# The head of an 8-core decoder-step kernel: x loads ungated, v's weights in two halves, v's norms in batches

## The reference, cut to what matters

```python
h = rmsnorm(x, g_mix)
proj = h @ w_in
a = proj[..., :o1]                      # pooling branch, 512 columns
z = jax.nn.gelu(proj[..., o1:o2])       # u and v, 512 columns each
u = z[..., :GMLP_WIDTH]
v = rmsnorm(z[..., GMLP_WIDTH:], g_v)
s = einsum('gij,bnjgc->bnigc', causal(w_s), vc) + b_s   # vc: v in chunks of 128 tokens
sg = u * s
```

## Time and profile before

| what | value |
|---|---|
| median of 3 runs | 831.54 us (831.36 to 833.17) |
| the profiled execution | 831.42 us |
| its span on the slowest core (core 2) | 829.6 us |
| spans of the 8 cores | 826.4 to 829.6 us |
| PE busy | 805.8 us, 97% of the span |
| DVE, ACT, POOL busy | 380.8, 225.0, 96.2 us |
| granted TensorE clock, by core | 0.993 to 0.999 |

### The profile page before, as it was taken

The page is one execution under the profiler, slowest core; times in us unless marked ns, Lnnn a source line. Parts: engine busy times, 40 slices in busy tenths (PEclk is TensorE's granted clock), DMA queues, the critical chain, the costliest instruction groups (busy, mean ns, idle before and its releaser), DMA issues.

```text
span 829.6 us, 12893 instructions; the slowest of 8 cores (826.4 to 829.6 us)
## 1 busy us (share of the span) xinstructions
PE 805.8 (97%) x4423; PEld 425.6 (51%) x4474; DVE 380.8 (46%) x618; ACT 225.0 (27%) x458; POOL 96.2 (12%) x154
## 2 busy tenths in 40 slices
PE   5999999999999999999999999999999999999996
PEld 3465666645666666644444444444444444444442
DVE  3776444468222222265776935446711111115357
ACT  2654322224211211120136352322321111110023
POOL 2720000012000000000312000011200000000001
PEclk9999999999999999999999999999999999999998
DMA  7894155684974543354977417688576444336313
GB/s 167 182 181 84 26 77 77 102 122 86 198 114 69 80 74 66 63 92 65 144 238 112 77 28 135 112 170 136 95 117 102 77 77 77 66 62 102 51 48 155
DMA packets 57315, 85.14 MB, mean 103 GB/s; under 512 B 23373, under 2 KB 23749, under 8 KB 57236
## 3 DMA queue, kind: packets, MB, share of 16 engines
q0 software_dynamic: 30352, 57.97, 45.3%
q1 hardware_dynamic: 26755, 26.09, 11.3%
q10 hardware_dynamic: 146, 0.27, 0.1%
HBM read 128.72 MB, written 9.01 MB: 166 GB/s over the span
## 4 chain that ended last, share of the span: by engine, by line
PE 84%; DVE 6%; issue 3%; DMA 2%; POOL 2%; ACT 2%; DVEq 0%; SPq 0%; POOLq 0%; ACTq 0%
PE ps L347 81%; DMA xbuf<-xp 2%; POOL rs L384 1%; DVE xbuf L367 1%; ACT junk L375 1%; ACT junk L992 1%; DVE xbuf L984 1%; PE ps L746 1%; PE ps L742 1%; DVE ybuf L1017 1%; DVE hb L404 0%; POOL rs L1003 0%; PE ps L695 0%; DVE shr L627 0%; DVE xbuf L874 0%
## 5 line engine op out<-in xcount | busy, mean ns | idle before, releaser
L347 PE MATMUL ps<-hT,ring 128*128 128x384 bf16 (+2 forms) x2698 | 484.1, 337 | 1.2
L347 PEld LDWEIGHTS ps<-hT,ring 128*128 128x128 bf16 x2720 | 265.5, 98 | 206.3
L347 PE MATMUL ps<-ring,ovl 128*128 128x512 bf16 x939 | 207.3, 379 | 1.1
L846 DVE TENSOR_TENSOR ovl<-ftmp,ps 128x384 bf16<-128x384 f32 (+2 forms) x110 | 64.2, 584 | 233.8 <-PE ps L347 226.5
L347 PEld LDWEIGHTS ps<-ring,ovl 128*128 128x128 bf16 x960 | 93.5, 98 | 113.8 <-issue 2.2
L844 ACT ACTIVATE ftmp<-ps 128x384 f32<-128x384 f32 (+2 forms) x110 | 56.3, 515 | 232.0 <-PE ps L347 232.0
L267 POOL DMA_DIRECT2D ring<-wpk x60 | 45.0, 750 | 493.8 <-PE ps L347 459.9
L944 DVE TENSOR_TENSOR xbuf<-xbuf,ps 128x512 f32<-128x512 f32 x64 | 43.4, 687 | 41.2 <-PE ps L347 41.1
L347 PE MATMUL ps<-ovl,ring 128*128 128x384 bf16 (+2 forms) x317 | 62.0, 337 | 0.2
L812 DVE TENSOR_TENSOR shr<-shr,ps 128x384 f32<-128x384 f32 (+2 forms) x40 | 23.4, 585 | 83.3 <-PE ps L347 74.5
L992 ACT ACTIVATE junk<-xbuf 128x512 bf16<-128x512 f32 (+1 forms) x34 | 21.3, 627 | 124.0 <-DVE xbuf L984 120.9
(11 more groups left out here) (90 smaller groups left out, 346.8 us busy)
## 6 DMA issues: line engine op xcount, KB each, us to landing
ring<-wpk POOLq DMA_DIRECT2D x48, 1024.0 KB, 11.2
xbuf<-xp SPq DMA_DIRECT2D x16, 512.0 KB, 6.6
yp<-ybuf SPq DMA_DIRECT2D x11, 512.0 KB, 3.4
ring<-wpk POOLq DMA_DIRECT2D x8, 512.0 KB, 13.0
ring<-wpk POOLq DMA_DIRECT2D x4, 768.0 KB, 8.1
yp<-shr SPq DMA_DIRECT2D x4, 512.0 KB, 2.6
AB<-xp SPq DMA_DIRECT2D x2, 512.0 KB, 6.9
shr<-xp SPq DMA_DIRECT2D x2, 512.0 KB, 11.6
```

The costliest lines, as they stand in the source:

```text
L347: ins = e.matmul(out=out, lhsT=lhs_fn(i), rhs=rhs_fn(i), start=(i == 0), stop=(i == n - 1))
L846: P.op('dve', lambda e: e.tensor_tensor(out=actT[:, f, c0:c0 + W], in0=ftmp[:, fi, :W], in1=PS[bU][:, :W], op=ALU.mult), reads=[('ftmp', f ...
```

## The change

In the head of pass 0, and in the layout of two weight blocks:

1. x: the loads of tiles 2 to 7 no longer wait for tile 1.
2. v's weights: block 0 is issued as two DMAs of half a block each (contraction chunks 0 to 3 and 4 to 7), both waiting for x of tile 0. The pieces are 2048 elements for block 0, 4096 for block 1, 1024 for the others, in both passes. Block 1 moves from i_ = 5 to i_ = 7, the small constants to i_ = 8, block 2 to i_ = 9.
3. v's matmuls: the first two tiles are done in halves of 4 matmuls, one step later than before (lag 4), so that the first half of tiles 0 and 1 comes ahead of the second half of either.
4. gelu writes v unscaled to `vg`, which lies where `mergedT` is later written (the sample tile's goes to `ftmp`), so no gelu waits for an L529. The squares follow from i_ = 9 on, POOL makes mean and power for three tiles in one instruction each, and DVE makes three tiles of `vtok` behind each.
5. The copies of `g_v` and the scalars move on DVE from before the loop to i_ = 3.

```diff
-WPIECE = 1024
+WPIECE = [2048 if i < 1 else 4096 if i < 2 else 1024 for i in range(len(WBLOCKS))]
...
+        def ring_issue_halves(j, after=()):
+            slot = j % NSLOT
+            off, ne = blocks[j]
+            for h_ in range(2):
+                dst = ring[:, slot, h_ * (ne // 2):(h_ + 1) * (ne // 2)]
+                src = wpk[0:1, off + h_ * 64 * ne:off + (h_ + 1) * 64 * ne].rearrange("o (p e) -> (o p) e", p=128)
+                P.dma('pool',
+                      (lambda e, dst=dst, src=src: e.dma_start(out=dst, in_=src)),
+                      'wh%d' % h_, reads=list(after), writes=[('ring', slot, h_)])
...
-            xload(0, slot, after=[('x', 1, 0)])
+            xload(0, slot)
...
-        ring_issue(0)
+        ring_issue_halves(0, after=[('x', 0, 0)])
...
+                def v_mm(t_):
+                    if t_ == 0:
+                        v_part(0, 0)
+                    elif t_ == 1:
+                        v_part(1, 0)
+                        v_part(0, 1)
+                    elif t_ == 2:
+                        v_part(1, 1)
+                        v_part(2, 0)
+                        v_part(2, 1)
...
+                vsq_at = {9: (0, 1), 10: (2, 3), 11: (4, 5), 12: (6,), 13: (7,), 14: (8,)}
+                vrs_at = {11: 0, 12: 3, 14: 6}
...
-                    at(i_ - 3, do_v)
+                    at(i_ - 4, v_mm)
...
-                    at(i_ - 7, lambda t_: vst[t_][2]())
...
+                    at(i_ - 5, v_gelu)
+                    for t_ in vsq_at.get(i_, ()):
+                        v_sq(t_)
+                    if i_ == 7:
+                        ring_issue(1)
+                    if i_ == 8:
                         late_pool_consts()
                         mid_sp_consts()
...
+                    if i_ in vrs_at:
+                        lo_ = vrs_at[i_]
+                        v_rs(lo_, lo_ + 3)
+                        for t_ in range(lo_, lo_ + 3):
+                            v_out(t_)
```

More of the change, by code:

```diff
@@ L472, in ws_prep @@
                      reads=['mask_f'], writes=[('wsT', g), ('ps', wb_)])
+        row_later = []
         def row_bcast(lo, n, dst, res, eng):
@@ L549, in build_nc @@
                 hst = [norm_stages(slot, R, col0, gmix_rep, 'gmix', copy_eng='dve') for (slot, R, col0) in hts]
-                vst = {}
                 n_ = len(hts)
+                kv = [newcol() for _ in range(n_)]
                 def at(t_, fn_):
@@ L555, in at, with v_dst, v_part, fn @@
                         fn_(t_)
-                def do_v(t_):
-                    vst[t_] = c_tile(*hts[t_], split=True)
+                def v_dst(t_):
+                    slot, R, col0 = hts[t_]
+                    return vg[:, slot, :] if slot < 8 else ftmp[:R, 0, :]
+                vbank = {}
+                def v_part(t_, h_, wv=wv):
+                    slot, R, col0 = hts[t_]
+                    if h_ == 0:
+                        vbank[t_] = bank()
+                        held.add(vbank[t_])
+                    b = vbank[t_]
+                    def fn(e, wv=wv):
+                        ins = None
+                        for i in range(4 * h_, 4 * h_ + 4):
+                            ins = e.matmul(out=PS[b][:R, :], lhsT=hT[:, i, col0:col0 + R], rhs=wv[:, i, :],
+                                           start=(i == 0), stop=(i == 7))
+                        return ins
+                    P.op('pe', fn, reads=[cres_[h_]] + hT_res([slot]), writes=[('ps', b)])
@@ new lines, in v_mm, with v_gelu @@
+                def v_mm(t_):
[8 more added lines that the diff above has]
+                        v_part(2, 1)
+                    else:
+                        v_part(t_, 0)
+                        v_part(t_, 1)
+                def v_gelu(t_):
+                    slot, R, col0 = hts[t_]
+                    b = vbank[t_]
+                    vd = v_dst(t_)
+                    P.op('act', lambda e: e.activation(out=vd, in_=PS[b][:R, :], func=AF.Gelu_apprx_tanh),
+                         writes=[('vg', slot), ('ps', b)] + ([('ftmp', 0)] if slot == 8 else []))
+                    held.discard(b)
@@ new lines, in v_sq, with v_rs @@
+                def v_sq(t_):
+                    slot, R, col0 = hts[t_]
+                    vd = v_dst(t_)
+                    k = kv[t_]
+                    ji = nxt('jk', 2)
+                    P.op('act', lambda e: e.activation(out=junk[:R, ji, 0:512], in_=vd, func=AF.Square,
+                                                       accum_out=ss[:R, k:k + 1]),
+                         reads=[('vg', slot)], writes=[('ss', k), ('junk', ji)])
+                def v_rs(lo, hi):
+                    ka, kb = kv[lo], kv[hi - 1] + 1
+                    P.op('pool', lambda e: e.tensor_scalar(out=ms[:, ka:kb], in0=ss[:, ka:kb], scalar1=1.0 / 512,
+                                                           scalar2=EPS, op0=ALU.mult, op1=ALU.add),
+                         reads=[('ss', k_) for k_ in range(ka, kb)], writes=[('ms', k_) for k_ in range(ka, kb)])
+                    P.op('pool', lambda e: e.tensor_tensor(out=rs[:, ka:kb], in0=ms[:, ka:kb],
+                                                           in1=mhalf[:, 0:1].to_broadcast([128, kb - ka]), op=ALU.pow),
+                         reads=[('ms', k_) for k_ in range(ka, kb)] + ['mhalf'],
+                         writes=[('rs', k_) for k_ in range(ka, kb)])
@@ new lines, in v_out @@
+                def v_out(t_):
+                    slot, R, col0 = hts[t_]
+                    vd = v_dst(t_)
+                    k = kv[t_]
+                    dst, dres = (vtok[:, slot, :], ('vtok', slot)) if slot < 8 else (vout[:, :], 'vout')
+                    P.op('dve', lambda e: e.scalar_tensor_tensor(
+                        out=dst, in0=vd, scalar=rs[:R, k:k + 1], in1=gv_rep[:R, :], op0=ALU.mult, op1=ALU.mult),
+                         reads=[('vg', slot), ('rs', k), 'gv'], writes=[dres] + ([('ftmp', 0)] if slot == 8 else []))
+                    if slot == 8:
+                        P.op('dve', lambda e: e.tensor_copy(out=vtok[:R, 8, :], in_=vout[:, :]),
+                             reads=['vout'], writes=[('vtok', 8)])
+                        P.dma('sp', lambda e: e.dma_start(out=nvs[:, :], in_=vout[:, :]), 'omisc', reads=['vout'])
@@ L559, in build_nc @@
+                vsq_at = {9: (0, 1), 10: (2, 3), 11: (4, 5), 12: (6,), 13: (7,), 14: (8,)}
+                vrs_at = {11: 0, 12: 3, 14: 6}
                 warm(10)
-                for i_ in range(n_ + 8):
-                    at(i_ - 3, do_v)
+                for i_ in range(n_ + 6):
+                    at(i_ - 4, v_mm)
                     at(i_ - 1, lambda t_: hst[t_][2]())
@@ L823, in build_nc @@
                             out=mergedT[:, d, c0:c0 + W], in0=gab[:, gi, 0, :W], in1=gab[:, gi, 1, :W], op=ALU.add),
-                             reads=[('gab', gi, 0), ('gab', gi, 1)], writes=[('mergedT', d, c0)])
+                             reads=[('gab', gi, 0), ('gab', gi, 1)],
+                             writes=[('mergedT', d, c0)] + ([('vg', t_) for t_ in range(9)] if s == 0 else []))
                         if s > 0 and carry['late']:
@@ L1155 @@
         np.concatenate([mats[n][:, c:c + m].reshape(k, 128, m).transpose(1, 0, 2).reshape(128, k * m)
-                        for (n, k, c, m) in blk], axis=1).reshape(128, -1, WPIECE).transpose(1, 0, 2).reshape(-1)
-        for blk in WBLOCKS]).reshape(1, WTOT)
+                        for (n, k, c, m) in blk], axis=1).reshape(128, -1, pc).transpose(1, 0, 2).reshape(-1)
+        for blk, pc in zip(WBLOCKS, WPIECE)]).reshape(1, WTOT)
     rows = np.zeros((1, 2048), dtype=np.float32)
```

35 lines of the change are left out of this document (20 added, 15 removed).

## The result

The changed kernel is slower: 837.13 us median (836.14 to 837.70, 4 runs) against 831.45 us for the kernel before in the same runs, ratio 1.007 (95% interval 1.0054 to 1.0086). The prediction was 827.4 us with a range to 831.0 us. The profiled execution took 836.14 us with a span of 834.6 us on core 2. The medians are over all executions, the ratios leave out the few that fell into a slower state of the chip (above 850 us). A difference between two kernels of different sets is taken from their ratios, 0.1% being 0.83 us.

The account below looks back on a forecast made before the run. PE, busy 97% of the span, was taken as the bound, so only its idle or half-pace time counts: 831.42 - 2.6 (earlier E) - 1.4 (spatial matmul wait) = 827.4 us, range 824.5 to 831.0 us.

Parts of the forecast that it names:

- E: Start of block 1's matmuls on PE, the head's end: forecast 39.4 us against 42.0 us, 2.6 us won.
- the bound of the tail: Block 0's second half in the head: last few weight packets, as on core 7 but moved 3.2 us, land by 22.4 us.
- The half pace: v's matmuls at half clock after PE idles: half of that price charged, 0.9 us.
- The estimate by equal turns: Weight and x packets alternating on the DMA engines: 16 turns of 0.56 us end at 17.7 us, between the bounds.
- The last product of v: End of the v chain behind the norms: begins at E + 4.9 us, 44.3 us, 4.3 us earlier than before.
- The 1.4 us at the spatial matmul: PE's wait for DVE at a spatial matmul: gone, since DVE comes 4.3 us earlier and PE 2.6 us; 1.4 us won.
- block 1, constants and block 2: Weight and constant loads behind x: block 1 issued at 25 us, landed at 35.2 us, 4 us ahead of E.
- Rival (a): Late weights' tail decides in the head: second half at 22.4 us, E about 41.9 us, 829.9 us in all; 16%.
- Block 2 is issued earlier: Issue of block 2's weights behind block 1: some 30 us against 38 us.
- (c): Block 1 late or its issue held up: PE waits until about 43.4 us, time 831.4 us; 7%.
- (b): All x tiles go ahead of the weights in the head: E = 46.0 us, time 834.1 us, slower; 11%.
- I take no gain: Larger weight pieces in the head: bounds half the transfer time and no gain, taken as no gain.

Follow-up runs that it names:

- b1_at5: The changed kernel with block 1 and the constants issued at i_ = 5 and block 2 at i_ = 8, as before: 828.02 us, ratio 0.9965.
- before_b1_late: The kernel before with block 1 and the constants moved from i_ = 5 to i_ = 7, block 2 left at i_ = 8: 839.58 us, ratio 1.0098.
- before_r2_early: The kernel before with block 2 issued right behind block 1 and the small constants (i_ = 5 instead of 8): 831.72 us, ratio 1.0008.
- w_at_once: The kernel of b1_at5 with the two halves of block 0 issued at once, not waiting for x of tile 0: 830.57 us, ratio 0.9989.
- r2_late: The changed kernel with block 2 issued after the loop, together with block 3: 838.43 us, ratio 1.0093.

## Why the prediction was wrong

**E, right in the sum.** Forecast 39.4 us on the slowest core, measured 39.6 (core 2) and 40.3 at most. Of its terms, the transposition of tile 2 came at 19.5 instead of 16.8 us, since PE waited for half 0 until 17.9 us (12.4 forecast), and half 1 let PE go on at 23.0 us (19.2 was free of cost, 22.4 the bound of the tail). Two other terms were too dear. The half pace was over by then (4 matmuls in 1.02 us at 23.01 us), 0.9 us not spent. And the 64 matmuls and 5 transpositions took 39.6 - 23.0 = 16.6 us, not 18.3: I had added durations that overlap, 1.90 and 0.62 us, where a tile with its transposition takes 2.17 us from start to start. So E came out right by luck, by errors that cancel: half 1 was 3.8 us later than the 19.2 us of the sum and also later than my outer bound of 22.4 us, and 2.6 us were charged that were not spent. The estimate by equal turns took 0.19 us of an engine for a weight packet; rows 7 give 6 x 16 x 1.021 / 414 = 0.24 us. Nothing in the sum hangs on it.

**The last product of v, right.** E + 4.9 us forecast, E + 5.0 measured; the power on 128x3 took 0.85 to 1.03 us, inside my bounds.

**The 1.4 us at the spatial matmul** were half there: 0.7 us of that wait are left on all cores of b1_at5. Yet the part behind E fell from 787.6 to 786.4 us, where I had forecast 786.2 us, so the sum behind E was nearly right; the wait of 0.4 us at L713 went as well, and one for `AB` fell from 1.0 to 0.7 us, neither of which I had counted. In the changed kernel other waits, ahead of it, hide this.

**The step that failed** is the one on block 1, constants and block 2: "an issue at 25 us against 26.45 us", "the mask and others behind it follow as before" and "Its cover is these 4 us". The issue came at 29.0 us, because half 1 was 3.8 us later than I took, and a chain hangs on it: v of tiles 0 and 1 on PE, ACT's gelu of tile 1, the square of x tile 6 behind it in ACT's stream, that tile's norm on POOL, and only then the issue. In the changed kernel, core 2:

```profile
25.67 0.59 ACT L613 ACTIVATE ovl<-ps 128x512 f32<-128x512 f32 x1
26.14 1.05 ACT L387 ACTIVATE junk<-xbuf 128x1024 bf16<-128x1024 f32 x1
...
28.47 0.55 POOL L396 TENSOR_TENSOR rs<-ms,mhalf 128x1 f32<-128x1 f32 x1
```

Rival (a) had that delay in it and priced only PE's wait. And I priced block 1 by its own landing: it did come nearly in time, the first matmul of block 1 waited 0.17 us. What I put at nothing is what stands behind it in the queues: the mask went out 3.0 us later than before and flew 12.9 us instead of 3.3. b1_at5 and before_b1_late show the price of that step, about 8.7 us one way and 8.1 us the other (of which some 1.5 us is the later E). With the step taken back, the kernel measures 828.0 us, where the rest of the sum said 827.4.

**"Block 2 is issued earlier"** was true (33.3 against 38.1 us) and worth nothing (before_r2_early: 0.9996 to 1.0020); I had not asked which loads it would then fly beside.

**Rivals.** (c) named block 1's late issue and stopped at "no change", with 7%, since it too counted one wait. (b) took place in neither form: x tiles and weights shared the engines. (a) and (b) joined a wait to the half pace that follows it, but only for v's weights, and no rival had a wait behind E with its half pace. The rule that (a) quotes from the Trainium skill, TensorE: Matmul & The Clock Gate, section HAM oscillation, half rate again after each wait for DMA, holds behind the long waits of the changed kernel (2.76 against 1.46 us for the same 8 matmuls), and not behind every short one: after the wait of 1.14 us at 23.01 us, 4 matmuls took 1.02 us, which is full pace.

**Pieces**: "I take no gain" was off by about 3.4 us, and the gate on tile 0 gained about 2 us by w_at_once; both were hidden in the E that came out right.

## What to carry to other kernels

Where the DMA engines are full for tens of microseconds behind the head, price a moved issue by the landing of every load behind it, each against the moment it is needed, and not by the landing of its own block. Idle engines ahead of the full stretch are the sign to look for: a late load that is cured shows the next one, and the gap is free only as long as all of them have cover. An issue on a compute engine's stream must not stand behind an operation that depends on an earlier load of the same kind; look for the chain load, matmul, gelu, norm, issue. A wait of PE cost about twice its length in the changed kernel, where PE came back at half pace.

## What the runs showed of the hardware

Weights that are converted on the way come in faster in larger pieces: with 2048 elements per piece for block 0 (and 4096 for block 1) against 1024, the second half of v starts at 21.6 to 22.8 us instead of 24.5 to 25.3 us, and the kernel is about 3.4 us faster. A 64 KB load of SP took 2.0 us in r2_late, where block 2 was not yet issued and the engines were busy for 65% of that time, and 11.2 to 13.8 us on the eight cores of the changed kernel, beside POOL's stream of 1 MB blocks (`ident_f`, as large: 17.5 us on core 2). Half pace followed PE's long waits (5.36 against 3.69 us for 24 matmuls behind 2.63 us) and not a wait of 1.14 us. Between 8 and 14 us, core 7 of the kernel before moved 414 weight packets to 17 of x, while with x ahead the two shared the engines (core 2 of b1_at5, 10 to 14 us, where its program is still that of the changed kernel):

```profile
q0 software_dynamic: 89, 0.36, 60.6%
q1 hardware_dynamic: 163, 0.60, 45.8%
```

What decides between the two kinds of sharing stays open.
